# A hybrid HGRN2, Hyena and ConvFFN step: the value projection split around the first head's tiles, the recurrence's steps four half products earlier

## The chip, the core and the metric

The kernel runs on one core of a Trainium2 chip. Its metric is the device time of one execution in microseconds (us). The engines of the core work side by side and wait for each other on semaphores: TensorE (PE, whose weight loads the profile counts as PEld), VectorE (DVE), ScalarE (ACT), GpSimd (POOL) and SyncE (SP), which issues most of the transfers.

## What is computed

One layer of a diffusion backbone over 640 tokens: 512 sample tokens (a grid of 8 rows of 64) and 128 prompt tokens, with width 1024, all in float32. Cut to what matters:

```python
mod = silu(cvec) @ ada_w + ada_b                    # sh1, sc1, g1, sh2, sc2, g2
h = rmsnorm(x, norm1_w) * (1 + sc1) + sh1
q, ff, fb, iv, g, hy = split(h @ w_in)              # 5 x 512 columns, then 3 x 512
# HGRN2, 4 heads of 128 x 128, forward and backward
S = diag(f) S + k v^T;  o = S^T q                   # f from ff or fb, v from iv
o_hg = rmsnorm_per_head(o_f + o_b) * hg_norm_w * silu(g)
# Hyena, 512 channels
v, x1, x2 = split(dwconv3(hy))
u = x1 * v;  z = long_conv(u, kern) + hy_d * u      # by a Fourier transform
y_hy = rmsnorm(x2 * z) * hy_norm_w
x = x + g1 * (concat(o_hg, y_hy) @ w_out)
h = rmsnorm(x, norm2_w) * (1 + sc2) + sh2
gate, val = split(dwconv3(h @ ffn_w_up))            # 2 x 2816 columns
x = x + g2 * ((silu(gate) * val) @ ffn_w_down)
y = rmsnorm(x, final_norm_w)
```

The outputs are `y` for both groups of tokens and the final states of the prompt's scans.

## The kernel before

**Products.** A float32 product is made of three passes with split operands: each operand is a high part (`_hi`) and the rest (`_lo`), and `split_product` (L1314 to L1316) multiplies high by high, low by high and high by low. A weight unit of 128 x 1024 comes into a ring of buffers `raw` by a transfer that SyncE issues (`fetch`, L487). ScalarE makes `w_hi` of it (`split_hi`, L577, the row L584) and VectorE `w_lo` (`split_lo`, L876, the row L884). There are four places for split units, so the split of unit n + 4 waits until TensorE is done with unit n. Each of the three engines runs a list of operations in an order written out by hand, and the calls of `split_hi` and `split_lo` are placed in it.

**Up to the second norm.** In the order of TensorE's list:
- The value projection (`token_major` at IV, L1437): token-major, four units with two products each for five tiles of 128 tokens, so 120 matmuls of 128 x 512 into the five banks of `V_BANKS`. ScalarE copies the banks to `vtok` (L683) when the last unit is done.
- The 28 input tiles of 128 columns, each in two half products of 320 tokens: half product n uses bank n % 3 and has 24 matmuls. For each of four heads a `q`, `ff`, `fb`, two `hy` and a `g` tile, and four `hy` tiles at the end. The recurrence of a head has 12 steps on TensorE (`step`, L1474), ScalarE (L685) and VectorE (`pass_k` L1039 and others); step j of head h stands behind half product 7 + 12h + j (`FIRST_STEP`, `step_at`, L438). Steps 0 to 6 are the levels of the scores, with keys `kc` copied by ScalarE (L690) and `QQ` and `KK` moved on by VectorE (L1063, L1048). The remaining adaLN products are also placed behind fixed half products (`ADA_QUAD`).
- The transposes of `u` (`turn_u`, L1533), its forward transform, the HGRN2 part of the output product, the inverse transform (four channels: eight products of a sample part, two of a prompt part that reads `Up`, L1627), with `sum_channels` (L1609) for the sums of squares, and the Hyena part of the output product (`mix`, L1639), a tile of tokens at a time.

**The second norm.** For each of five tiles of 128 tokens: VectorE adds the residual (`mix_tile`, L1214, three operations on 128 x 1024), ScalarE squares and roots (`norm_tile`, L788), VectorE takes the reciprocal (`norm_row`, L1227 on), ScalarE scales to `xn` (`scale_tile`, L795), TensorE transposes in eight pieces (`turn_tile`, L1658), ScalarE modulates the eight pieces to `hf` (`modulate_tile`, L803), and VectorE splits them (`split_tile`, L894).

**The FFN.** Three rounds of 8, 8 and 6 tiles of 128 columns for gate and value. A round has for each unit two half products (`ffn_halves`, L123, which gives the order; in the first round the first halves of the first three units come ahead of their second halves), on banks 5 to 7; ScalarE takes each out to `padf` (`spread`, L589 to L594), VectorE convolves (L903 on), multiplies and splits. Behind them are two down projections, token-major, of five banks each, which VectorE adds to `x` (`add`, L1255: the rows L1257 and L1258). `before_half` (L1679) says what TensorE waits for, or does, ahead of one of the first half products. Between down projections TensorE's first product into bank i waits for the add of bank i:

```python
for k in range(nf // 2):
    split_lo(unit + LEAD_FFN)
    unit += 1
for i in range(NT):
    eng.wait_ge(sem("down_made"), (2 * r + n) * NT + i + 1)
    add(i, n, "down_taken", "x1_ready")
```

## Time and profile before

| | |
|---|---|
| median of three runs | 989.09 us (986.1 to 990.16) |
| the profiled execution | 991.46 us |
| its span, first to last instruction | 989.7 us |
| mean granted TensorE clock | 0.983 |
| PE busy | 941.6 us (95%), 5588 matmuls |
| PEld busy | 828.3 us (84%) |
| DVE busy | 629.1 us (64%) |
| ACT busy | 347.4 us (35%) |
| POOL busy | 14.1 us (1%) |
| DMA | 99.06 MB, mean 100 GB/s |

A share of busy time is an average over stages with different limits. TensorE is busy nearly throughout, so the time can change by what is left of its idle time, by the clock that it is granted (1.00 is 2.4 GHz, 0.50 is 1.2 GHz), and by the number of its instructions. The list of what it waited for tells which engine's order ended each wait.

The stages in the trace, in us from the span's start: the value projection 78.9 to 106.9, the 56 half products with the recurrence from 106.9, the HGRN2 part of the output product 414.3 to 442.0, the inverse transform from 445.0, the Hyena part of the output product to 488.6, the first FFN half product at 502.8, and the last adds, the final norm and the stores to 989.7.

### The profile page before, as it was taken

How to read it: one execution, taken by the hardware profiler on the slowest of the kernel's cores; microseconds unless marked ns; L12 is line 12 of the kernel's file. 1: busy time of each engine (PE TensorE's matmuls, PEld its weight loads, DVE VectorE, ACT ScalarE, POOL GpSimd, SP SyncE). 2: the span in 40 equal slices, each digit the busy share in tenths (PEclk: the TensorE clock that was granted, in tenths of full speed). 3: DMA queues.
4: the chain of work that ended last, by engine and by line, in shares of the span. 5: the costliest groups of instructions: out<-in, count | busy, mean ns of one | idle time of the engine just before them, and what ended most of it. 6: DMA issues, size and time to landing. Idle time of an engine off the chain costs nothing.

```text
span 989.7 us, 13758 instructions
## 1 busy us (share of the span) xinstructions
PE 941.6 (95%) x5588; PEld 828.3 (84%) x5588; DVE 629.1 (64%) x811; ACT 347.4 (35%) x614; POOL 14.1 (1%) x25
## 2 busy tenths in 40 slices
PE   6789999999999999989879999989999998999996
PEld 1247999899889899578769999878999986899985
DVE  4875258596695786896665766443756644466655
ACT  2362434333433333232473333211343321133332
POOL 0000000000000000001000000000000000000000
PEclk9899999999999999999989999999999999999998
DMA  8545144324422443115031221212122132112102
GB/s 284 217 175 167 65 150 128 101 77 149 134 97 100 129 128 123 64 43 192 1 126 66 86 86 65 91 58 85 65 72 78 64 106 65 64 64 86 43 1 106
DMA packets 27366, 99.06 MB, mean 100 GB/s; under 512 B 3271, under 2 KB 3655, under 8 KB 26536
## 3 DMA queue, kind: packets, MB, share of 16 engines
q1 hardware_dynamic: 25240, 89.06, 26.6%
q0 software_dynamic: 2064, 9.13, 2.7%
q8 instruction: 44, 0.72, 0.3%
q14 instruction: 18, 0.15, 0.1%
HBM read 95.01 MB, written 3.16 MB: 99 GB/s over the span
## 4 chain that ended last, share of the span: by engine, by line
PE 83%; DVE 10%; ACT 4%; issue 2%; DMA 1%; SPq 0%; DVEq 0%; ACTq 0%
PE ps L1314 23%; PE ps L1316 23%; PE ps L1315 23%; PE ps L1491 4%; PE ps L1332 2%; PE ps L1351 1%; PE ps L1627 1%; ACT hf L809 1%; DMA raw<-in_slots 1%; PE ps L1503 1%; PE ps L1586 1%; DVE h_lo L892 1%; DVE w_lo L884 1%; PE ps L1342 1%; PE ps L1511 1%
## 5 line engine op out<-in xcount | busy, mean ns | idle before, releaser
L1314 PE MATMUL ps<-h_hi,w_hi 128*128 128x320 f32 x1152 | 362.5, 315 | 3.7 <-DVE w_lo L884 3.7
L1315 PE MATMUL ps<-h_lo,w_hi 128*128 128x320 f32 x1152 | 357.6, 310 | 0.0
L1316 PE MATMUL ps<-h_hi,w_lo 128*128 128x320 f32 x1152 | 357.6, 310 | 0.0
L884 DVE TENSOR_TENSOR w_lo<-raw,w_hi 128x1024 fp32r<-128x1024 f32 x106 | 129.7, 1225 | 151.3 <-ACT w_hi L584 147.1
L1314 PEld LDWEIGHTS ps<-h_hi,w_hi 128*128 128x128 f32 x1152 | 218.2, 189 | 6.1 <-issue 4.3
L1315 PEld LDWEIGHTS ps<-h_lo,w_hi 128*128 128x128 f32 x1152 | 218.1, 189 | 0.1
L1316 PEld LDWEIGHTS ps<-h_hi,w_lo 128*128 128x128 f32 x1152 | 217.8, 189 | 0.0
L584 ACT ACTIVATE w_hi<-raw 128x1024 fp32r<-128x1024 f32 x106 | 111.2, 1052 | 119.6 <-PE ps L1316 114.5
L1314 PE MATMUL ps<-w_hi,a_hi 128*128 128x512 f32 x220 | 86.7, 394 | 6.3 <-DVE tmpd L1257 6.3
L1315 PE MATMUL ps<-w_lo,a_hi 128*128 128x512 f32 x220 | 86.4, 393 | 0.0
L1316 PE MATMUL ps<-w_hi,a_lo 128*128 128x512 f32 x220 | 86.2, 392 | 0.0
L1314 PEld LDWEIGHTS ps<-w_hi,a_hi 128*128 128x128 f32 x220 | 41.7, 189 | 16.4 <-issue 7.1
L903 DVE TENSOR_SCALAR cf<-padf,vec 128x648 f32<-128x648 f32 x44 | 24.5, 556 | 40.7 <-ACT padf L594 40.6
L1316 PEld LDWEIGHTS ps<-w_hi,a_lo 128*128 128x128 f32 x220 | 41.7, 190 | 8.8
L1315 PEld LDWEIGHTS ps<-w_lo,a_hi 128*128 128x128 f32 x220 | 41.7, 189 | 8.4
L1314 PE MATMUL ps<-w_hi,h_hi 128*128 128x512 f32 x120 | 48.1, 401 | 0.0
L1316 PE MATMUL ps<-w_hi,h_lo 128*128 128x512 f32 x120 | 46.8, 390 | 0.0
L1315 PE MATMUL ps<-w_lo,h_hi 128*128 128x512 f32 x120 | 46.7, 389 | 0.0
L851 ACT ACTIVATE a_hi<-actf 128x640 fp32r<-128x640 f32 x22 | 16.3, 741 | 80.1 <-DVE actf L1285 80.1
L1491 PEld LDWEIGHTS ps<-QQ,kc 128*128 128x128 f32 x280 | 35.9, 191 | 10.1 <-issue 10.1
L1491 PE MATMUL ps<-QQ,kc 128*128 128x128 f32 x280 | 39.3, 288 | 2.7 <-issue 2.7
L904 DVE SCALAR_TENSOR_TENSOR cf<-padf,vec,cf 128x648 f32<-128x648 f32 x44 | 39.3, 894 | 1.6
(254 smaller groups left out, 1047.8 us busy)
## 6 DMA issues: line engine op xcount, KB each, us to landing
raw<-in_slots SPq DMA_DIRECT2D x154, 512.0 KB, 3.7
xin<-in_x_sample SPq DMA_DIRECT2D x4, 512.0 KB, 5.8
xres<-in_x_sample POOLq DMA_DIRECT2D x4, 512.0 KB, 5.1
grow<-gates POOLq DMA_DIRECT2D x2, 1024.0 KB, 6.9
out_y_sample<-x SPq DMA_DIRECT2D x4, 512.0 KB, 3.1
decay<-in_decay SPq DMA_DIRECT2D x1, 1280.0 KB, 12.0
ktab<-in_ktab SPq DMA_DIRECT2D x1, 1024.0 KB, 5.7
tab<-in_utab POOLq DMA_DIRECT2D x1, 1024.0 KB, 7.5
```

Source lines behind the costliest of these rows:

```text
L584: A(w_hi[:, n % SPLITS, :], src, ACT.Copy).then_inc(sem("hi_ready"), 1)
L809: last = A(hf2[:, i % 2, k * P:(k + 1) * P], ps[:, TURN_BANKS[i] + k // 4, k % 4 * P:(k % 4 + 1) * P], ACT.Identity, scale=gain[:, 1, k, s ...
L851: A(a_hi[:, f, :], actf[:, :], ACT.Copy).then_inc(sem("ahi_ready"), 1)
L884: V.tensor_tensor(w_lo[:, n % SPLITS, :], raw[:, r % RING, :], w_hi[:, n % SPLITS, :].bitcast(F32), ALU.subtract).then_inc(sem("lo_ready"), 1)
L892: link(V.tensor_tensor(h_lo[:, k, :], buf, h_hi[:, k, :].bitcast(F32), ALU.subtract), "h_split")
L903: link(V.tensor_scalar(out, pad[:, 1:1 + CONV], taps[1], None, ALU.mult))
L904: link(V.scalar_tensor_tensor(out=out, in0=pad[:, 0:CONV], scalar=taps[0], in1=out, op0=ALU.mult, op1=ALU.add))
L1314: mm(out, lhs[0], rhs[0], start=first, stop=False)
L1315: mm(out, lhs[0], rhs[1], start=False, stop=False)
L1316: return mm(out, lhs[1], rhs[0], start=False, stop=last)
L1332: last = mm(ps[g * GROUP:(g + 1) * GROUP, bank, :], silu_c[:, GROUPS * j + g, :], piece[:, g % 2 * HW:(g % 2 + 1) * HW], start=(j == 0), s ...
L1491: last = mm(chunk(j, c), kc[:, l % 2, c * P:(c + 1) * P], ap(QQ, c * P, [(2 * s, P // (2 * s)), (T + s, 2), (1, s)]), start=True, stop=True)
```

## The change

Everything is done by the same arithmetic in the same numbers; what moves is the order on the engines, with the banks and semaphores that this needs.

- The value projection is made in two parts (`value_units`): units 0 and 1, then the six half products of head 0's `q`, `ff` and `fb`, then units 2 and 3, in which steps 0 to 2 of head 0 stand (`FIRST_AT`). The steps of all heads move up by four half products (`FIRST_STEP` 7 to 3). Head 0 has no `hy` tiles; six of them stand at the end, and the transposes of `u` stand between these.
- The adaLN products behind half products move along (`ada_half`).
- The inverse transform has its sample and prompt parts apart (`z_sample`, `z_prompt`); the sample parts of the first channels stand ahead of what reads `Up`, and the sums of squares stand later. VectorE makes the last two splits of the output weights behind the chain of `Up`.
- The second norm has another order on all three engines. For tiles 1, 2 and 4 VectorE takes four of the eight modulated pieces (`modulate_rest`). `mix` of tiles 3 and 4 is done in two halves of the columns. ScalarE squares into a buffer of its own (`junk2`).
- The first FFN round begins with the first halves of four units instead of three.
- In each down projection VectorE's last split of a weight unit stands behind the five adds.

The core of the diff:

```diff
 HY_TILES = [3 * _c + _what for _c in range(NC) for _what in (0, 1)] + [3 * _c + 2 for _c in range(NC)]
+_at_hy = iter(HY_TILES)
...
-    TILES += [("q", _g), ("ff", _g), ("fb", _g), ("hy", HY_TILES[2 * _g]), ("hy", HY_TILES[2 * _g + 1]), ("g", _g)]
-TILES += [("hy", _i) for _i in HY_TILES[2 * HEADS:]]
+    TILES += [("q", _g), ("ff", _g), ("fb", _g)] + [("hy", next(_at_hy)) for _ in range(2 if _g else 0)] + [("g", _g)]
+TILES += [("hy", _i) for _i in _at_hy]
...
-FIRST_STEP = 7
+FIRST_STEP = 3
+HEAD_TILES = 3
+HEAD_STEPS = 2 * HEAD_TILES - FIRST_STEP
...
-    first = 3 if r == 0 else 0
+    first = 4 if r == 0 else 0
     return [(u, half) for half in range(2) for u in units[:first]] + [(u, half) for u in units[first:] for half in range(2)]
...
+def tile_unit(t):
+    return IV // 2 + t if t < HEAD_TILES else IV + t
+IV_UNITS = (0, 1, HEAD_TILES + 2, HEAD_TILES + 3)
...
-    i = e - ADA_EARLY
-    return 5 + 12 * (i // 2) + 5 * (i % 2)
+    i = e - ADA_EARLY + 1
+    return 1 + 12 * (i // 2) + 5 * (i % 2)
...
+            def first_steps():
+                split_hi(8)
+                for j in range(HEAD_STEPS):
+                    step(0, j)
+                    if j == 1:
+                        split_hi(9)
+                for i in range(NT):
+                    eng.wait_ge(sem("v_bank"), i + 1)
+                    A(vtok[:, i, :], ps[:, V_BANKS[i], :], ACT.Copy).then_inc(sem("v_ready"), 1)
...
             for n in range(NH):
+                if n == 2 * HEAD_TILES:
+                    first_steps()
+                if n > FIRST_TURN:
+                    take_u(n - FIRST_TURN - 1)
                 kind, i = TILES[n // 2]
                 half = n % 2
                 c0 = half * HT
...
+                  scale=knorm[:, 1, c:c + 1]).then_inc(sem("z_taken"), 1)
+                eng.wait_ge(sem("zp_made"), c + 1)
...
+        junk2 = sb(norm2, "junk2", [D])
...
-                for k in range(KD):
+                if i >= 2:
+                    eng.wait_ge(sem("h_split"), KD + i - 1)
+                for k in range(KD // 2 if i in SHARED else KD):
...
             norm_tile(0)
             scale_tile(0)
             norm_tile(1)
-            scale_tile(1)
             modulate_tile(0)
             norm_tile(2)
+            scale_tile(1)
             scale_tile(2)
             modulate_tile(1)
+            split_hi(UNIT_FFN)
             modulate_tile(2)
-            split_hi(UNIT_FFN)
+            split_hi(UNIT_FFN + 1)
             norm_tile(3)
+            split_hi(UNIT_FFN + 2)
             scale_tile(3)
-            split_hi(UNIT_FFN + 1)
+            eng.wait_ge(sem("padf_zero"), 1)
+            take_half(NH, 0, 0, 0)
+            norm_tile(4)
+            split_hi(UNIT_FFN + 3)
             modulate_tile(3)
-            norm_tile(4)
             scale_tile(4)
-            split_hi(UNIT_FFN + 2)
+            take_half(NH + 1, 0, 1, 0)
             modulate_tile(4)
-            split_hi(UNIT_FFN + 3)
-            eng.wait_ge(sem("padf_zero"), 1)
...
+                if n == 2 * HEAD_TILES - 1:
+                    split_lo(8)
+                    for j in range(HEAD_STEPS):
+                        pass_k(0, j)
+                        step(0, j)
+                        if j == 1:
+                            split_lo(9)
...
-            for k in range(2):
-                split_lo(UNIT_WOUT + 4 + k)
...
+            for k in range(2):
+                split_lo(UNIT_WOUT + 4 + k)
...
+            def modulate_rest(i):
+                s = int(i == NT - 1)
+                eng.wait_ge(sem("x_turned"), 2 * i + 2)
+                for k in range(KD // 2, KD):
+                    link(V.tensor_scalar(hf2[:, i % 2, k * P:(k + 1) * P], ps[:, TURN_BANKS[i] + 1, k % 4 * P:(k % 4 + 1) * P],
+                                         gain[:, 1, k, s:s + 1], mod[:, 3 * KD + k, s:s + 1], ALU.mult, ALU.add),
+                         "h_rest" if k == KD - 1 else None)
...
             mix_tile(0)
+            mix_tile(1)
             norm_row(0)
-            mix_tile(1)
+            mix_tile(2)
             norm_row(1)
-            mix_tile(2)
             split_tile(0)
             norm_row(2)
+            modulate_rest(1)
+            modulate_rest(2)
+            split_tile(1)
+            split_lo(UNIT_FFN)
+            split_tile(2)
+            split_lo(UNIT_FFN + 1)
             mix_tile(3)
-            split_tile(1)
-            split_tile(2)
-            split_lo(UNIT_FFN)
+            split_lo(UNIT_FFN + 2)
             norm_row(3)
             mix_tile(4)
-            split_lo(UNIT_FFN + 1)
+            split_lo(UNIT_FFN + 3)
+            norm_row(4)
             split_tile(3)
-            norm_row(4)
-            split_lo(UNIT_FFN + 2)
+            modulate_rest(4)
             split_tile(4)
-            split_lo(UNIT_FFN + 3)
...
-                    for k in range(nf // 2):
+                    for k in range(nf // 2 - 1):
                         split_lo(unit + LEAD_FFN)
                         unit += 1
...
                         if last_half and 0 < i < NT - 1:
                             final_norm(i - 1)
+                    split_lo(unit + LEAD_FFN)
+                    unit += 1
...
+        FIRST_AT = ((2, 3), (3, 1), (3, 4))
...
+            def first_steps(p, i):
+                if (p, i) in FIRST_AT:
+                    step(0, FIRST_AT.index((p, i)))
...
+            def value_units(ps0, after):
+                for p in ps0:
+                    hi, lo = unit_ready(IV_UNITS[p])
+                    for i in range(NT):
+                        for kk in range(2):
+                            k = 2 * p + kk
+                            before_v(p, i, k)
+                            last = split_product(ps[:, V_BANKS[i], :], [x[:, k, i * P:(i + 1) * P] for x in (h_hi, h_lo)],
+                                                 [x[:, kk * HW:(kk + 1) * HW] for x in (hi, lo)], k == 0, k == KD - 1)
+                        if p == IV - 1:
+                            last.then_inc(sem("v_bank"), 1)
+                        elif i == NT - 1:
+                            last.then_inc(sem("unit_done"), 1)
+                        after(p, i)
...
+            value_units((0, 1), lambda p, i: None)
             for n in range(NH):
-                if n < 3:
-                    eng.wait_ge(sem("v_ready"), V_BANKS.index(n) + 1)
-                else:
+                if n == 2 * HEAD_TILES:
+                    value_units((2, 3), first_steps)
+                if 2 * HEAD_TILES <= n < 2 * HEAD_TILES + 3:
+                    eng.wait_ge(sem("v_ready"), V_BANKS.index(half_bank(n)) + 1)
+                elif n >= 3:
                     eng.wait_ge(sem("half_free"), n - 2)
-                if n == 3:
+                half_product(n, tile_unit(n // 2), n % 2)
...
+                if n == FIRST_TURN:
                     eng.wait_ge(sem("u_ready"), NC)
+                    eng.wait_ge(sem("rms_ready"), HEADS)
...
+            eng.wait_ge(sem("up_ready"), 1)
+            z_sample(0)
+            z_sample(1)
+            z_prompt(0)
+            z_sample(2)
+            z_prompt(1)
+            z_sample(3)
+            eng.wait_ge(sem("raw_taken"), 2 * NT)
+            sum_channels(0)
+            z_prompt(2)
+            sum_channels(1)
+            z_prompt(3)
...
             mix(2)
             turn_tile(0)
-            eng.wait_ge(sem("ysum_ready"), 1)
-            mix(3)
+            mix(3, (0,))
+            eng.wait_ge(sem("h_full"), KD + 1)
+            mix(4, (0,))
             turn_tile(1)
             turn_tile(2)
-            eng.wait_ge(sem("h_full"), KD + 1)
-            mix(4)
+            mix(3, (1,))
+            mix(4, (1,))
 
...
-                if at in (0, 3):
-                    eng.wait_ge(sem("h_split"), KD + (3, 5)[at // 3])
+                if at == 0:
+                    eng.wait_ge(sem("h_split"), KD + 3)
                 if at == 1:
-                    turn_tile(3)
                     eng.wait_ge(sem("mixed_taken"), 4)
                 if at == 2:
+                    turn_tile(3)
+                if at == 3:
                     turn_tile(4)
+                if at == 4:
+                    eng.wait_ge(sem("h_split"), KD + NT)
```

**VectorE at the first down projection's boundary** (`w_lo` is a weight split, `tmpd` and `x` are the two operations of an add). Before:

```order
L1284 TENSOR_TENSOR actf<-cf 128x512
L1285 TENSOR_TENSOR actf<-cf 128x128
L1287 TENSOR_TENSOR a_lo<-actf,a_hi 128x640
L884 TENSOR_TENSOR w_lo<-raw,w_hi 128x1024 x5
L1257 TENSOR_TENSOR tmpd<-ps,grow 128x512
L1258 TENSOR_TENSOR x<-x,tmpd 128x512
```

Now:

```order
L1341 TENSOR_TENSOR actf<-cf 128x512
L1342 TENSOR_TENSOR actf<-cf 128x128
L1344 TENSOR_TENSOR a_lo<-actf,a_hi 128x640
L922 TENSOR_TENSOR w_lo<-raw,w_hi 128x1024 x4
L1314 TENSOR_TENSOR tmpd<-ps,grow 128x512
L1315 TENSOR_TENSOR x<-x,tmpd 128x512
```

Four more pairs of adds follow in both. The first of the splits in the row belongs to the last unit of the half products; one of the others has moved behind the adds.

**VectorE in the second norm** (L1222 or L1266 is the first operation of a mix tile, L898 or L936 of a split tile, the reciprocal that of a norm). From the third mix tile on, before:

```order
L1222 SCALAR_TENSOR_TENSOR x<-ps,rhy,x 128x2x512
L1224 TENSOR_TENSOR x<-x,grow 128x2x512
L1225 TENSOR_TENSOR x<-x,xres 128x2x512
L898 CAST h_hi<-hf 128x8x128
L899 TENSOR_TENSOR h_lo<-hf,h_hi 128x8x128
L1230 RECIPROCAL stat<-stat 128x1
L1222 SCALAR_TENSOR_TENSOR x<-ps,rhy,x 128x2x512
```

Now:

```order
L1266 SCALAR_TENSOR_TENSOR x<-ps,rhy,x 128x2x512
L1268 TENSOR_TENSOR x<-x,grow 128x2x512
L1269 TENSOR_TENSOR x<-x,xres 128x2x512
L1274 RECIPROCAL stat<-stat 128x1
L936 CAST h_hi<-hf 128x8x128
L937 TENSOR_TENSOR h_lo<-hf,h_hi 128x8x128
L1274 RECIPROCAL stat<-stat 128x1
L1285 TENSOR_SCALAR hf<-ps,gain,mod 128x128 x8
L936 CAST h_hi<-hf 128x8x128
L937 TENSOR_TENSOR h_lo<-hf,h_hi 128x8x128
L922 TENSOR_TENSOR w_lo<-raw,w_hi 128x1024
```

The fourth mix tile stood behind one split; it now stands behind three splits of tiles, eight modulated pieces and two weight splits (the rows go on with the third split, a `w_lo` and the mix tile), and a third `w_lo` stands between it and its reciprocal.

**ScalarE at the value projection** (`vtok` are the value banks' copies, `qs` the first of head 0's `q`, `TT` and `KK` its gates and keys, `kc` the keys of a level). Before:

```order
L584 ACTIVATE w_hi<-raw 128x1024 x5
L683 ACTIVATE vtok<-ps 128x512 x5
L584 ACTIVATE w_hi<-raw 128x1024
L721 ACT_TABLE_LOAD
L721 ACTIVATE qs<-ps 128x320 x2
L584 ACTIVATE w_hi<-raw 128x1024
```

Now, from the last gate of head 0 on:

```order
L764 ACTIVATE TT<-ps 128x320
L765 ACTIVATE KK<-ps 128x320
L604 ACTIVATE w_hi<-raw 128x1024
L707 ACTIVATE kc<-KK 128x640 x2
L604 ACTIVATE w_hi<-raw 128x1024
L707 ACTIVATE kc<-KK 128x640
L735 ACTIVATE vtok<-ps 128x512 x5
L604 ACTIVATE w_hi<-raw 128x1024
L758 ACT_TABLE_LOAD
L758 ACTIVATE gs<-ps 128x320
```

The copies of the value banks stood ahead of head 0's tiles; they now stand behind the keys of its first three levels.

## Rows read from the trace of the kernel before

**Rows 1.** What PE waited for: us in total, times, longest

```profile
PE ps L1314 <- DVE tmpd L1257: 6.3, 2, 3.2
PE ps L1662 <- ACT xn L800: 5.1, 2, 2.7
...
PE ps L1314 <- DVE w_lo L884: 3.7, 2, 2.4
...
PE ps L1627 <- DVE Up L1180: 2.9, 1, 2.9
```

**Rows 2.** Windows: us, busy PE, PEld, DVE, ACT, POOL, granted clock, DMA, GB/s

```profile
445.03:450.04 5.01, 5.01 (x16) 4.20 (x17) 0.00 (x0) 0.00 (x0) 3.13 (x6) 0.70 0.68 238
450.49:453.94 3.45, 3.45 (x18) 3.04 (x17) 2.08 (x4) 1.18 (x3) 0.00 (x0) 1.00 1.05 430
502.82:507.88 5.06, 5.06 (x24) 5.06 (x25) 4.92 (x4) 2.06 (x2) 1.00 (x2) 0.68 0.32 104
...
517.20:625.55 108.35, 108.35 (x721) 108.35 (x721) 68.82 (x84) 41.17 (x82) 0.00 (x0) 0.97 0.24 78
685.00:797.63 112.63, 112.63 (x769) 112.63 (x768) 74.18 (x92) 39.24 (x77) 0.00 (x0) 1.00 0.22 71
625.55:652.94 27.39, 27.39 (x122) 22.34 (x120) 9.05 (x10) 5.37 (x7) 0.00 (x0) 1.00 0.29 96
656.10:685.00 28.90, 28.90 (x121) 23.77 (x121) 9.79 (x12) 3.18 (x3) 0.00 (x0) 0.94 0.22 73
828.18:855.78 27.60, 27.60 (x121) 22.29 (x121) 9.78 (x12) 3.18 (x3) 0.00 (x0) 1.00 0.24 77
```

**Rows 3.** Timeline at a down boundary: start, length, engine, [idle before, releaser]

```profile
654.12 1.23 DVE L884 TENSOR_TENSOR w_lo<-raw,w_hi 128x1024 fp32r<-128x1024 f32 x1 [5.57 <-ACT w_hi L584]
655.27 0.68 DVE L1257 TENSOR_TENSOR tmpd<-ps,grow 128x512 f32<-128x512 f32 x1
...
656.10 0.63 PE L1314 MATMUL ps<-w_hi,a_hi 128*128 128x512 f32 x1 [3.16 <-DVE tmpd L1257]
```

**Rows 4.** Timeline of DVE ahead of the inverse transform

```profile
437.83 2.36 DVE L884 TENSOR_TENSOR w_lo<-raw,w_hi 128x1024 fp32r<-128x1024 f32 x2
```

**Rows 5.** Timeline of DVE, the first channel of the inverse transform

```profile
451.75 0.89 DVE L1199 SCALAR_TENSOR_TENSOR zc<-u_hy,vec,zc 128x640 f32<-128x640 f32 x1 [6.87 <-ACT zc L777]
...
455.82 1.23 DVE L884 TENSOR_TENSOR w_lo<-raw,w_hi 128x1024 fp32r<-128x1024 f32 x1
```

**Rows 6.** Timeline of DVE, last mix tile to last split tile

```profile
502.78 1.28 DVE L1222 SCALAR_TENSOR_TENSOR x<-ps,rhy,x 128x1024 f32<-128x1024 f32 x1
...
506.62 1.22 DVE L884 TENSOR_TENSOR w_lo<-raw,w_hi 128x1024 fp32r<-128x1024 f32 x1
...
512.19 1.23 DVE L899 TENSOR_TENSOR h_lo<-hf,h_hi 128x1024 fp32r<-128x1024 f32 x1
```

**Rows 7.** Timeline of ACT, last tile of the second norm

```profile
513.64 1.15 ACT L800 ACTIVATE xn<-x,stat 128x1024 f32<-128x1024 f32 x1 [0.86 <-DVE stat L1230]
...
515.65 2.88 ACT L809 ACTIVATE hf<-ps,mod,gain 128x128 f32<-128x128 f32 x8
```

**Rows 8.** Groups of DVE: busy us, mean ns of one | idle before

```profile
L1079 DVE SCALAR_TENSOR_TENSOR states<-states,TU,ps 128x128 f32<-128x128 f32 x16 | 5.6, 348 | 0.6
```

**Rows 9.** Timeline, first convolution of the FFN and fifth unit's first half

```profile
527.72 0.56 DVE L903 TENSOR_SCALAR cf<-padf,vec 128x648 f32<-128x648 f32 x1 [5.95 <-ACT padf L594]
...
549.97 0.42 ACT L589 ACTIVATE padf<-ps 128x320 f32<-128x320 f32 x1
```

**Rows 10.** Timeline of DVE, head 0's first levels

```profile
145.51 1.42 DVE L1063 TENSOR_TENSOR QQ<-QQ,TT 128x640 f32<-128x640 f32 x1
...
148.73 0.83 DVE L1048 TENSOR_TENSOR KK<-KK,TU 128x640 f32<-128x640 f32 x1
```

**Rows 11.** Timeline of ACT: a value bank's copy, a level's keys

```profile
101.74 0.60 ACT L683 ACTIVATE vtok<-ps 128x512 f32<-128x512 f32 x1 [0.30 <-PE ps L1316]
...
149.59 0.74 ACT L690 ACTIVATE kc<-KK 128x640 f32<-128x640 f32 x1 [1.19 <-DVE KK L1048]
```

More of the change, by code:

```diff
@@ L111 @@
 NSLOT = _s
-UNIT_TILE = IV
 UNIT_WOUT = IV + len(TILES)
@@ L200, in token_major @@
         out.append((name, value))
-    token_major(IV, "v_bank", NT)
-    out.extend(("half_made", 2 * t + 2) for t in range(len(TILES)))
+    halves = [("half_made", 2 * t + 2) for t in range(len(TILES))]
+    out += [("unit_done", 1), ("unit_done", 2), *halves[:HEAD_TILES], ("unit_done", 3), ("v_bank", NT), *halves[HEAD_TILES:]]
+    plain = IV - 1
     out.extend(("hg_mixed", NT * (n + 1)) for _, n, _ in WOUT_UNITS[:4])
@@ L811, in modulate_tile, with take_half @@
                 last.then_inc(sem("h_full"), 1)
+            def take_half(n, t, gv, half):
+                eng.wait_ge(sem("half_made"), n + 1)
+                if t >= 2 and half == 0:
+                    eng.wait_ge(sem("fconv"), 2 * (t - 2) + gv + 1)
+                spread(ps[:, half_bank(n), 0:HT], padf[:, t % 2, gv, :], half, "half_free")
             norm_tile(0)
@@ L838, in _ @@
                     t = t0 + f
[L839 to L842 removed]
+                    if n >= NH + 2:
+                        take_half(n, t, gv, half)
                     n += 1
```

154 lines of the change are left out of this document (73 added, 81 removed).

## The prediction

> **What bounds the kernel now.** I read the list of what TensorE waited for first: nearly all of its idle time behind the first 60 us stands in four lines [rows 1]. Two waits of 3.2 us are for the first add of a down projection; the transposes of the second norm wait 2 x 2.7 us at most for `xn`; the first FFN products wait for `w_lo`; the inverse transform waits 2.9 us for `Up`. Elsewhere TensorE is fed, so nothing that only moves work there can gain. The windows [rows 2] add what a wait costs afterwards: sixteen inverse-transform products take 5.01 us at a granted clock of 0.70 behind their wait, where the next sixteen and their neighbours take 3.45 at 1.00. Behind the two down waits the same 120 products take 28.90 (0.94) and 27.60 (1.00) against 27.39 for the half before. So a wait may or may not bring the lower of the clock's two levels (1.2 GHz), and costs 0.2 to 1.7 us more. The rest is read where the waits are: VectorE's own order of work.
>
> I sum against the profiled execution, 991.46 us with a span of 989.7; it lies 2.4 above the median of 989.09, so the difference is taken over to the median. About 0.5% (5 us) can be told from no change.
>
> **1. The two down boundaries.** VectorE makes the `w_lo` of four units and then does the adds. The last unit's slot is free only when TensorE has finished the half, so `w_lo` starts at 654.12, the first add at 655.27 and TensorE at 656.10 [rows 3]. With the last `w_lo` behind the adds, the adds start while the last unit is still being multiplied: a product is 27.39/120 = 0.228 us, a tile of the last unit six, 1.37; a pair of adds is 1.44 (twice 0.69 and two gaps), so the adds keep up to within 1 us and never hold the next half, which takes its banks 1.37 apart. The moved `w_lo` is wanted four units (27 us) later: nothing. Saved: twice 3.16 plus 0.17 of overlap with the product before, and 1.5 and 0.2 of slow clock (28.90 and 27.60 less 27.39, and 0.17 each since the first half's end laps over): 5.0 + 3.7 = **8.7**. The third round's second half has no such wait, and saves nothing. Bounds: 6.7 (the waits alone) and 10.0 (both followed by the slow level).
>
> **2. The inverse transform.** The channels' first product no longer waits for `Up`. VectorE has its last input at 437.8 [rows 4], TensorE is in the output product until 441.97 (the start at 445.03 less the 2.9 wait and the overlap), so the products start 3.1 earlier and at full clock. That is not what comes out: the prompt part of channel 0 now stands behind two channels of products, 441.97 + 2 x 3.45 + 0.5 = 449.3, and ScalarE's copy 0.6 later. VectorE's channel then runs from 449.95, where it ran from 451.75 [rows 5]: 1.8 earlier. A channel is 4.0 of VectorE, and the first two carry a `w_lo` of 1.2 (451.75 to 455.82 and 1.23): 18.3 in all, so the fourth `y_split` comes at 468.2. TensorE waits for the third and fourth (1.2 and 1.4), and the sums of squares end at 470.75; VectorE's first mix tile starts at 472.1, which was 473.5: **1.4** net, of 3.1 in sight.
>
> **3. The second norm, up to the FFN.** A mix tile is 3.84 of VectorE (502.78 to 506.62), a split tile 1.96 (0.69 and the 1.23 of the row) [rows 6]; on ScalarE `xn` takes 1.15, eight modulate pieces 2.88 [rows 7], square and root 1.5 (from the tile's end to `xn` less the waits). Mix tiles 0 and 1 now run back to back, tile 2 ends at 485.6, and its norm no longer waits for a split. `modulate_rest` puts four pieces per shared tile on VectorE at 0.36 (0.35 and a gap, the nearest VectorE operation on a 128 x 128 piece of PSUM [rows 8]). The split of tile 2 ends at 497.8, and the first half product starts at 497.9, where it started at 502.82 [rows 2]. Then it turns: mix tile 3 ends at 502.85, but VectorE's next `w_lo` (third FFN unit) waits until ScalarE has done norm 3 and then this unit's `w_hi` (505.3), and the norm's reciprocal stands behind it, at 506.75. `xn` 3 is there at 508.0: TensorE, with two half products done at 504.9, waits 3.1. The same again: mix tile 4 to 510.6, norm 4, `w_hi`, eight pieces, `xn` 4 at 517.05: TensorE waits 4.7 more, the fourth half product starts at 517.9 (the third started at 517.20), the last split ends at 521.5 and the fifth half starts between 521.5 and 523 by the clock; I take 522.4.
>
> What the Trainium skill says against this part: "Advanced Engine Details and Errata", TRN2 Errata, has VectorE and ScalarE pay their memory latency as a bubble between instructions, advises large tiles, and puts ScalarE closer to PSUM; by it, four small pieces from PSUM are dearer on VectorE than on ScalarE, and at twice the price three shared tiles would add 4.3 us to VectorE's chain. The trace does not bear this out: 0.348 a piece on VectorE [rows 8] against 2.88/8 = 0.36 on ScalarE [rows 7].
>
> **4. The FFN's lead-in.** With four first halves instead of three, four units come to their convolutions 3.5 us apart. From the first convolution to the taking of the first half of the fifth unit VectorE and ScalarE need 549.97 - 527.72 = 22.25 us [rows 9]. From the fifth half's start at X the convolution starts at X + 4.2 and that half is taken by X + 26.9; TensorE wants its bank at X + 24.6 (seven times 3.52, which is 112.63/32 [rows 2]): a new wait of **2.3**. Twenty-one halves follow: the round's halves end at 522.4 + 26.9 + 73.9 = 623.2. Before: 625.55. Parts 2 to 4 together: **-2.35**. Bounds: -5.5 (no slow clock, X = 521.5, and no lead-in wait) and +1.5 (two spells of slow clock inside the waits' tails).
>
> **5. The value projection and head 0.** TensorE's instructions are the same, in another order; the split weights of both parts are made while three tiles run. Steps 0 to 2 of head 0 fit their slots: `qk_next` comes 4.5 after the last half product, the slot at 5.4. But ScalarE now copies level 2's `kc` before the five value banks, and that waits for VectorE: level 0 (148.73 - 145.51 = 3.2 [rows 10]), a `w_lo` of 1.2, then `pass_k` 0.83 [rows 10], from the end of step 1. That is 5.3, plus `kc` 0.74 and the first copy 0.60 [rows 11]: 6.7. TensorE has three value tiles (4.1) and step 2 (1.2) in that time, and half product 6 needs that copy: **+1.7**, a wait that was not there before. Bounds: 0, and 3.4 with a slow spell of 1.7.
>
> **6. The rest of the shift.** Head 0 has two tiles fewer and the steps start four halves sooner, so for each later head the steps meet the same tiles as before; the ada products keep their places beside the steps. The six last hyena tiles bring VectorE some 41 us of work in twelve slots of four: covered. The transposes of `u` now stand between half products; before they stood partly behind the last one, but TensorE was fed there too. The joins still wait for the last half product. 0, and if that cover were gone, up to 1 us per head.
>
> Sum: -8.7 - 2.35 + 1.7 = -9.35, so 989.09 - 9.35 = **979.7**.
>
> **The rivals.**
> A, the forecast: 979.7. Chance 0.5.
> B, the second norm's stage gains more: VectorE's chain is as I have it, but no slow clock follows the longer waits and the lead-in wait is hidden. For it: 27.60 at full clock behind a wait of 3.2 us [rows 2]. Against: two of three such waits were followed by the slow level. -8.7 - 5.5 + 1.7: 976.6. Chance 0.2.
> C, only the down boundaries gain, and the new waits of parts 3 to 5 (1.7, 3.1, 4.7, 2.3) cost what parts 2 and 3 give and a slow spell more: -8.7 + 1.5 + 1.7 = -5.5: 983.6. Chance 0.2.
> D, the shift does more than it says: ending the recurrence four halves early takes VectorE's last head off the way to the joins, where it stood at the end (a reciprocal of the whole head). Against: the joins wait for TensorE's tables product. At most 4 us more, the length of that reciprocal: 975.7. Chance 0.05.
> E, slower than before: the clock. The change makes many short waits of few long ones; I count eight (0.8, 1.2, 1.4, 1.7, 1.9, 2.3, 3.1, 4.7). The round-0 stretch in which two stood ran its 30 halves in 108.35 at 0.97 where 105.6 would be full speed: 2.8 lost behind one spot. If six of the eight cost that much and none is hidden by the chain it waits for, +16.8 - 9.35: 996.5; it decides from four on (11.2 against 9.35), slower by over 0.5% from six. Against: the longest two are tails of VectorE's chain, which a slow product only fills. Chance 0.05.
>
> **How the numbers follow.** Faster by over 0.5% (below 984.1): A, B, D and most of C: 0.88. Within 0.5%: the rest of C and the mild end of E: 0.08. Slower: 0.04. Range: A's terms move by 1.3 at the boundaries, by 3 in the norm, by 1.7 at the values, and B and C lie within: 975.5 to 984.5. Outside are E and the ends of C and D.
>
> **What would show it.** Right: no wait for the add of the down projection in TensorE's list; no wait for `Up`; a wait of some 1.7 us of TensorE for `vtok` before half product 6; two waits for `xn` of about 3 and 4.7 us with the fourth half product at its old place; one wait of 2 us for `padf` in the FFN's first ten halves. Wrong: waits per step of the recurrence, a down boundary that still waits, or a granted clock well under 0.98 over the run.

## The result, and the profile after

| | before | changed |
|---|---|---|
| median | 988.91 us (4 runs, 986.1 to 990.16) | 1000.58 us (4 runs, 996.47 to 1002.27) |
| the profiled execution | 991.46 us, span 989.7 | 999.02 us, span 997.2 |
| mean granted clock in it | 0.983 | 0.984 |
| PE busy | 941.6 us | 947.5 us |

The ratio is 1.0112, 95% interval 1.0069 to 1.0156: **slower by 1.1%**, where 979.7 was forecast and nothing above 984.5 was in the range. Below, what TensorE waited for in the changed kernel (the list of waits; us in total, times, longest), the answer to [rows 1]:

```profile
PE ps L1664 <- DMA tab<-in_utab: 7.7, 1, 7.7
PE ps L1761 <- ACT xn L829: 5.6, 2, 4.4
...
PE ps L1373 <- DVE h_lo L937: 2.5, 1, 2.5
PE ps L1373 <- ACT padf L609: 2.2, 1, 2.2
...
PE ps L1373 <- ACT vtok L735: 1.3, 1, 1.3
```

The waits for the adds and for `Up` are gone. At the top stands a wait that the kernel before did not have: the first product of the forward Fourier transform of `u` waits 7.7 us for its table, a transfer that GpSimd issues. The stages as windows of the changed kernel (columns as in [rows 2]): up to the HGRN2 part of the output product, that product, on to the first FFN product, the first round's half products, its two down projections, the second round, its down projections, the rest; then the transform and the fourth FFN half product.

```profile
81.70:429.36 347.66, 334.64 (x2219) 298.47 (x2217) 227.75 (x289) 121.84 (x194) 9.67 (x13) 0.99 0.33 109
429.36:457.01 27.65, 27.65 (x123) 22.69 (x121) 26.72 (x29) 8.31 (x12) 0.00 (x0) 1.00 0.16 57
457.01:514.62 57.61, 54.37 (x266) 45.88 (x264) 42.64 (x66) 24.91 (x50) 3.15 (x6) 0.94 0.28 105
514.62:641.85 127.23, 119.40 (x784) 118.64 (x785) 82.33 (x100) 50.06 (x99) 1.05 (x2) 0.96 0.23 86
641.85:696.28 54.43, 54.43 (x242) 45.07 (x241) 24.83 (x30) 9.61 (x11) 0.00 (x0) 1.00 0.25 87
696.28:808.92 112.64, 112.64 (x770) 112.64 (x768) 70.24 (x87) 39.23 (x77) 0.00 (x0) 1.00 0.20 71
808.92:863.34 54.42, 54.42 (x242) 45.05 (x241) 24.84 (x30) 9.62 (x11) 0.00 (x0) 1.00 0.25 87
863.34:997.20 133.86, 125.46 (x757) 118.08 (x755) 81.36 (x105) 44.85 (x94) 0.00 (x0) 0.99 0.16 59
411.82:428.21 16.39, 16.39 (x33) 7.29 (x34) 7.38 (x7) 2.74 (x4) 0.00 (x0) 0.85 0.06 23
535.20:541.00 5.80, 5.80 (x28) 5.80 (x27) 3.56 (x6) 1.49 (x6) 0.00 (x0) 0.63 0.00 0
```

The same stages of both kernels, each from TensorE's first instruction to the next stage's, give where the 7.5 us between the two spans come from:

| stage | before | changed | difference |
|---|---|---|---|
| up to the value projection | 79.02 | 81.70 | +2.68 |
| value projection to the HGRN2 output product | 335.31 | 347.66 | **+12.35** |
| that product to the first down projection | 211.22 | 212.49 | +1.27 |
| down projections, first round | 59.45 | 54.43 | -5.02 |
| half products, second round | 112.63 | 112.64 | 0.0 |
| down projections, second round | 58.15 | 54.42 | -3.73 |
| the rest | 133.92 | 133.86 | -0.06 |

The first row isn't the change's: two early groups of four products each took 3.8 us where they took 2.0, and so they did in one profiled execution of an unchanged start (the eleventh run below begins its value projection at 82.08, the third, the same kernel, at 79.06). The second row is the loss. GpSimd's list there (its timeline) is, in the kernel before:

```profile
366.83 1.79 POOL L540 DMA_DIRECT2D gates<-mod  x2 [46.06 <-DVE mod L947]
377.18 0.56 POOL L529 DMA_DIRECT2D tab<-in_utab  x1 [8.55 <-PE ps L1498]
385.24 0.71 POOL L529 DMA_DIRECT2D out_new_state<-newst  x1 [7.50 <-DVE newst L1083]
393.50 0.58 POOL L529 DMA_DIRECT2D ptab<-in_ptab  x1 [7.55 <-PE ps L1520]
```

and in the changed kernel:

```profile
394.86 1.80 POOL L560 DMA_DIRECT2D gates<-mod  x2 [86.12 <-DVE mod L985]
396.64 0.56 POOL L549 DMA_DIRECT2D tab<-in_utab  x1
397.20 0.71 POOL L549 DMA_DIRECT2D out_new_state<-newst  x1
397.90 0.58 POOL L549 DMA_DIRECT2D ptab<-in_ptab  x1
```

Ahead of the table's load stands the store of the second residual gate, two transfers of 1024 elements of 4 bytes (the expectation of run 1 says 512), which waits for the last adaLN block (`mod`). Before, the gate was out 10 us ahead of what the table itself waits for, the last head's step 8. Now that step is done early, but the last adaLN block comes 28 us later. The load is issued at 396.64 and lands 15.1 later, where TensorE had been ready at 404.1. The transform that follows ran at a granted clock of 0.85: 16.39 us.

### The profile page after: what moved, and what is told of

Its sections match the earlier page's. It is cut to its first block, busy times and chain, and to the rows that moved or that the text cites. A ratio compares the mean times of both kernels' runs of the same rounds, so it can differ in the third digit from the quotient of the medians.

```text
span 997.2 us, 13758 instructions
## 1 busy us (share of the span) xinstructions
PE 947.5 (95%) x5588; PEld 831.0 (83%) x5588; DVE 634.2 (64%) x823; ACT 342.1 (34%) x602; POOL 14.1 (1%) x25
## 4 chain that ended last, share of the span: by engine, by line
PE 80%; DVE 11%; ACT 3%; DMA 3%; issue 2%; POOL 0%; SPq 0%; ACTq 0%; DVEq 0%
PE ps L1373 22%; PE ps L1375 22%; PE ps L1374 21%; PE ps L1566 3%; PE ps L1391 2%; PE ps L1410 2%; PE ps L1664 2%; DMA tab<-in_utab 2%; PE ps L1705 1%; DMA raw<-in_slots 1%; DVE w_lo L922 1%; DVE o_hg L1126 1%; PE ps L1578 1%; DVE h_lo L930 1%; ACT hf L840 1%
## 5 line engine op out<-in xcount | busy, mean ns | idle before, releaser
L1566 PEld LDWEIGHTS ps<-QQ,kc 128*128 128x128 f32 x280 | 35.9, 191 | 10.5 <-issue 10.3
## 6 DMA issues: line engine op xcount, KB each, us to landing
decay<-in_decay SPq DMA_DIRECT2D x1, 1280.0 KB, 10.4
tab<-in_utab POOLq DMA_DIRECT2D x1, 1024.0 KB, 15.1
```

The costliest lines, as they stand in the source:

```text
L1566: last = mm(chunk(h, j, c), kc[:, l % 2, c * P:(c + 1) * P], ap(QQ, c * P, [(2 * s, P // (2 * s)), (T + s, 2), (1, s)]), start=True, stop= ...
```

## The experiments

Each ratio is to runs of the kernel before on the same chip. Three theories at first: **Q**, the loss is GpSimd's queue, in which the table's load stands behind the store; **S**, the shift itself would put another wait at the same place; **C**, the loss is many short waits and the clock behind them. The runs stand here by what they test, numbered as they were made.

**1. The gate's store behind the tables.**

```diff
-            gate_out(1)
             eng.wait_ge(sem("head_steps"), (HEADS - 1) * STEPS + KTURN + 1)
...
             load(ptab[:, :, :, :], io["ptab"][:, 1:3], "ld_ptab")
+            gate_out(1)
```

> The changed kernel with one move on GpSimd's list: the store of the second gate (two transfers of 512 elements each, wait for the last adaLN block) stands behind the loads of the Fourier table and of the prompt's table, not ahead of them. Theory Q (the queue): the changed kernel loses its time because the table's load stands behind that store in GpSimd's list; it was issued at 396.6 and landed at 411.8, TensorE had been ready at 404.1, waited 7.7 us and made the transform at a granted clock of 0.85 (16.4 us where 13.8 would do). By Q the wait for the table is gone and the run is 10.3 shorter than the changed kernel: 990 by its median of 1000.6, 987 by its profiled run. Theory S (the shift itself: the last head's end or the splits take over as the next wait at the same place): a new wait of 5 us or more ahead of the second part of the transform, 996 to 998. Theory C (many short waits and the clock, no single place): within 2 us of the changed kernel, 999 to 1001.

Measured: 988.23, ratio 0.9962 (0.9937 to 0.9988), span 989.6. GpSimd's timeline, and the window from the transform to the output product:

```profile
365.41 0.59 POOL L549 DMA_DIRECT2D tab<-in_utab  x1 [56.63 <-PE ps L1572]
...
394.93 1.77 POOL L560 DMA_DIRECT2D gates<-mod  x2 [10.23 <-DVE mod L984]
```

```profile
403.99:419.04 15.05, 15.05 (x38) 6.68 (x37) 10.82 (x11) 4.13 (x8) 0.57 (x1) 1.00 0.15 30
```

The table is issued 31 us earlier and no wait takes its place. From the value projection to the output product: 337.08 against 347.66, 10.6 shorter, 7.7 of it the wait and 2.5 the clock (17.54 against 15.05 from the transform's start). Q holds for this stage (it had 10.3), S and C fall. The whole profiled execution is 7.6 shorter, not 10.6: between the output product and the first FFN half product it took 59.90, where the changed kernel's took 57.61 in the same order.

**2. The wait kept, the gate's packets behind the table's load.**

```diff
-            gate_out(1)
-
+            eng.wait_ge(sem("mod_ready"), ADA_ORDER.index(11) + 1)
             eng.wait_ge(sem("head_steps"), (HEADS - 1) * STEPS + KTURN + 1)
             eng.wait_ge(sem("scores_taken"), HEADS * 8)
             load(tab[:, :].rearrange("p (a b c d) -> p a b c d", a=2, b=2, c=2), io["utab"], "ld_tab")
+            gate_out(1)
```

> The changed kernel, with GpSimd still waiting for the last adaLN block ahead of the table's load, but with the store of the gate (1024 elements of 4 bytes) issued behind that load. It splits theory Q in two. If the gate's small packets ahead in the same queue made the table's landing take 15.1 us where it took 7.5 in the kernel before: the table is issued at about 395 and lands at 402.5, just ahead of TensorE's 404.1, so the time is that of the first run of this job (990 or 987). If the landing was slow for another reason (other traffic): it lands at 410, TensorE waits 6 us, and the time is within 2 us of the changed kernel's.

Measured: 994.89, ratio 1.0037 (1.0016 to 1.0058), between the two times that were expected. The load was issued at 392.15 and landed at 407.1; TensorE waited 5.7. So that the packets stand ahead in the queue is not what makes the landing slow.

**5. The wait kept, the store far away** (behind the inverse table's load).

```diff
-            gate_out(1)
-
+            eng.wait_ge(sem("mod_ready"), ADA_ORDER.index(11) + 1)
             eng.wait_ge(sem("head_steps"), (HEADS - 1) * STEPS + KTURN + 1)
...
             load(tab[:, :].rearrange("p (a b c d) -> p a b c d", a=2, b=2, c=2), io["itab"], "ld_tab")
+            gate_out(1)
```

> The changed kernel, with GpSimd waiting for the last adaLN block ahead of the Fourier table's load as in the changed kernel, but with the gate's store (1024 elements of 4 bytes) far away, behind the load of the inverse table. In the run with the store right behind the table's load the load still took 15.0 us, so its order in the queue was not what made it slow. Theory N (the small packets near it, before or behind, take the engines' time): the table, issued at 392 to 395, lands in 5 to 7.5 us, by 402, TensorE (ready at 401.5 to 404) waits under 1 us, and the ratio to the kernel before is that of the run with the store behind the tables, 0.996. Theory W (the wait alone, with whatever else moves at that time): it lands after 15 us, TensorE waits 5 to 6, ratio 1.003.

Measured: 985.81, ratio 0.9972 (0.994 to 1.0004); the load, issued at 394.66, landed in 8.0, and TensorE didn't wait. The view of the transfers in the 7.4 us behind the load's issue in the changed kernel, and in the 8 us behind it here:

```profile
DMA packets 134, 0.31 MB, mean 42 GB/s; under 512 B 80, under 2 KB 80, under 8 KB 115
...
tab<-in_utab POOLq DMA_DIRECT2D x1, 1024.0 KB, 15.1
raw<-in_slots SPq DMA_DIRECT2D x1, 512.0 KB, 13.8
```

```profile
DMA packets 466, 2.20 MB, mean 275 GB/s; under 512 B 60, under 2 KB 60, under 8 KB 337
...
tab<-in_utab POOLq DMA_DIRECT2D x1, 1024.0 KB, 8.0
raw<-in_slots SPq DMA_DIRECT2D x1, 512.0 KB, 5.0
```

Runs 2 and 5 differ in the place of the store alone, and the landing is 14.9 in one and 8.0 in the other. The slow spell comes a few us behind the store and takes SyncE's load of a weight in another queue too (13.8 against 5.0). In run 2 the 8 us behind the load's issue still carried 217 GB/s, and the 7 us after them (400 to 407) 48:

```profile
DMA packets 390, 1.73 MB, mean 217 GB/s; under 512 B 100, under 2 KB 100, under 8 KB 261
```

```profile
DMA packets 103, 0.33 MB, mean 48 GB/s; under 512 B 22, under 2 KB 22, under 8 KB 103
```

A load that has moved by then is spared: in run 5 the inverse table's load, 1 MB too, was issued 0.55 us ahead of the store and landed in 5.4. A load of SyncE's that came 3.1 us behind the store took 9.8. That the elements of 4 bytes are the cause is argued and not shown, since no run stores the gate in another form; a store as such isn't enough, for that of the last state, 128 KB, was issued 0.6 us behind the table's load in run 5 too.

The two halves of the fault are needed together: the wait put the load late by 29 us, for which there was just room, and the gate's packets beside it took 7 us more. The store beside an early load was not run; the table of run 1 landed over 33 us ahead of its use, which would hide it. The Trainium skill says on its page "DMA: Bandwidth & Descriptors", section "Queues, rings and completion order", that each DMA engine takes turns between queues packet by packet. That a load in another queue is slowed as well is in keeping with it.

**4. The fault alone, in the kernel before.**

```diff
+            eng.wait_ge(sem("head_steps"), HEADS * STEPS)
             gate_out(1)
-
-            eng.wait_ge(sem("head_steps"), (HEADS - 1) * STEPS + KTURN + 1)
```

> The kernel before with the fault alone: on GpSimd's list the wait for the last head's last step (393.0 in its trace) stands ahead of the gate's store and of the table's load. By theory Q the table is issued at 395, lands at 410 behind the gate's packets, TensorE waits 11 us from 398.8 on and loses some 2.6 to the clock: 1002.5. If the wait in the changed kernel was only a sign of something else that TensorE would have waited for anyway: 989 to 992.

Measured: 1003.28, ratio 1.0121 (1.0084 to 1.0158); a wait of 10.3 for the table, and 18.23 us from the transform to the output product where the kernel before has 15.49. Q again, with its price.

**3. The adds first, in the kernel before.**

```diff
-                    for k in range(nf // 2):
+                    for k in range(nf // 2 - 1):
...
+                    split_lo(unit + LEAD_FFN)
+                    unit += 1
```

> The kernel before with one part of the change: in each down projection VectorE's last split of a weight unit stands behind the five adds. By the forecast's own term: 8.7 less, 980.2 by the median of 988.9, with no wait for an add in TensorE's list. A rival: the boundary's time comes back later (the split that is made late, or a first half product that waits for it): 2 us or less gained, 987.

Measured: 983.04, ratio 0.9918 (0.9895 to 0.9941), 8.1 less. Its windows for the two pairs of down projections:

```profile
626.02:680.45 54.43, 54.43 (x243) 45.05 (x242) 24.84 (x30) 9.62 (x11) 0.00 (x0) 1.00 0.26 87
793.08:847.50 54.42, 54.42 (x242) 45.05 (x241) 24.83 (x30) 9.62 (x11) 0.00 (x0) 1.00 0.27 87
```

They are those of the changed kernel to 0.01 us, and nothing comes back later: the profiled span is 8.3 shorter.

The next five stand on run 1. One caution for all of them: the stretch from the inverse transform's start to the first FFN half product, in which they have one order, took 59.9 in runs 1, 2, 5, 6 and 12, but 58.24, 56.64, 56.72 and 56.66 in runs 7 to 10. Runs 9 and 12 are the same kernel, so up to 3 us there come from the execution and not from the edit.

**6. Value copies first.**

```diff
-                for j in range(HEAD_STEPS):
+                for j in range(HEAD_STEPS - 1):
                     step(0, j)
-                    if j == 1:
-                        split_hi(9)
+                split_hi(9)
                 for i in range(NT):
+                    if i == NT - 1:
+                        step(0, HEAD_STEPS - 1)
```

> The changed kernel with the gate's store behind the tables (the first run of the first job, 0.996 of the kernel before), and ScalarE's copies of the first four value banks ahead of the keys of head 0's level 2. By the forecast's part 5: TensorE's wait of 1.3 for a value bank ahead of the seventh half product is gone, 1.3 less, ratio 0.995, which is at the edge of what can be told, so the profile decides: value projection to the start of the HGRN2 output product 1.3 shorter. A rival: the keys come later and step 2 of head 0 waits in its place: same time.

Measured: 985.7, ratio 0.997 (0.9947 to 0.9994), not to be told from run 1 by time; the window from the value projection to the output product is 335.25 where run 1 has 337.08, and the wait for `vtok` is gone: 1.8.

**7. Another order in the second norm.**

```diff
             split_hi(UNIT_FFN + 1)
-            norm_tile(3)
             split_hi(UNIT_FFN + 2)
+            split_hi(UNIT_FFN + 3)
+            norm_tile(3)
             scale_tile(3)
...
-            norm_tile(4)
-            split_hi(UNIT_FFN + 3)
             modulate_tile(3)
+            norm_tile(4)
...
-            mix_tile(3)
             split_lo(UNIT_FFN + 2)
+            mix_tile(3)
+            split_lo(UNIT_FFN + 3)
             norm_row(3)
             mix_tile(4)
-            split_lo(UNIT_FFN + 3)
-            norm_row(4)
             split_tile(3)
+            norm_row(4)
```

> The changed kernel with the gate's store behind the tables (0.996 of the kernel before), and another order in the second norm: ScalarE splits the third and fourth FFN unit ahead of the norm of tile 3, VectorE the third ahead of mix tile 3 and the fourth ahead of its reciprocal, ScalarE modulates tile 3 ahead of the norm of tile 4. Theory O (the stage's lost gain is order on ScalarE and VectorE: two reciprocals stand behind a split that waits for a split on ScalarE): the waits of 1.2 and 4.4 for xn fall to 0.2 and 1.8, the fifth half product starts 5 earlier, ratio 0.991. A rival (the adds and splits of tiles on VectorE are the bound, whatever their order): 1 to 2 less, 0.9945.

Measured: 983.53, ratio 0.9931 (0.9901 to 0.996). From the inverse transform to the first down projection 183.07 (58.24 + 124.83) against 187.50 (59.90 + 127.60) in run 1: 4.4 less, of which 1.7 lie ahead of the first half product, where the order is the same, and 2.8 behind it. The waits for `xn` are 1.6 and 2.6, not 0.2 and 1.8: the two half products ahead of the first ran at full clock here (7.37 us, not 8.8), so TensorE was there sooner, and at the second VectorE's reciprocal stood behind the split of tile 3. So order gave some 2.8 us here, between the 5 and the 1 to 2 that were expected; by time the gain isn't clear, since the interval of run 6, on the same chip and without this order, overlaps (0.9947 to 0.9994).

**8. Runs 6 and 7 together.**

> The two before this together: gate's store behind the tables, value copies first, and the other order in the second norm. If their gains add: 1.3 + 5 less than the run with the store alone moved, ratio 0.990, which is below the kernel before with the adds first alone (0.992).

Measured: 983.05, ratio 0.9939 (0.9908 to 0.9971), short of the 0.990 expected and no better than run 7 by time. Its stages are 335.33, which is the gain of run 6, and 179.93, 3.1 below run 7 in the same order; half of that again lies ahead of the first half product.

**9. VectorE takes half of tile 3's pieces too** (on run 8).

```diff
-        SHARED = (1, 2, 4)
+        SHARED = (1, 2, 3, 4)
...
             mix_tile(4)
-            split_tile(3)
+            modulate_rest(3)
             norm_row(4)
+            split_tile(3)
```

> The run with the store behind the tables, value copies first and the other order in the second norm, and now VectorE also takes four of the eight modulated pieces of tile 3, right behind mix tile 4. In that run ScalarE was still at tile 3's pieces when mix tile 4 was ready, and TensorE waited 2.6 for xn of tile 4. If that ScalarE time is what it waited for: the wait falls to 1.1 and the fifth half product starts 1.5 earlier, ratio 0.001 to 0.002 below that run's 0.994. If VectorE's four pieces (0.44 each with the gap) hold the split of tile 3 and with it the fifth half product: no change in the end of the first round's half products.

Measured: 981.52, ratio 0.9887 (0.9854 to 0.9919). The longest wait for `xn` is 1.6, and that for tile 4 1.3; the wait that was to shrink did. The first half product to the first down projection took 122.62 against 123.29, but 121.09 in run 12, the same kernel, so those 0.7 can't be told from the spread.

**10. Three first halves** (on run 8).

```diff
-    first = 4 if r == 0 else 0
+    first = 3 if r == 0 else 0
...
                 if at == 3:
                     turn_tile(4)
-                if at == 4:
                     eng.wait_ge(sem("h_split"), KD + NT)
```

> The run with the store behind the tables, value copies first and the other order in the second norm, with three first halves instead of four in the first FFN round, as in the kernel before. By the forecast's part 4 the wait for padf of 2.2 ahead of the twelfth half product is the price of four first halves: it is gone here; in its place TensorE waits for the split of tile 4 ahead of the fourth half product, some 4 (split at 522.8 where it is at 518.9). Net 1.5 to 2 longer from the first half product to the first down projection. If the padf wait stays, part 4 read its cause wrongly.

Measured: 985.04, ratio 0.9916 (0.9884 to 0.9947), and 126.24 against 123.29 in that window, 2.95 longer. From its list of waits:

```profile
PE ps L1373 <- DVE h_lo L937: 6.4, 2, 3.9
```

No wait for `padf` is left in it, and one of 3.9 for the split of tile 4 has come: part 4 of the forecast read the cause rightly. By this window four first halves are worth their price; by time that isn't shown (run 8 has 0.9939).

**11 and 12. The adds alone beside the best version.** Run 11 is the kernel of run 3, run 12 that of run 9.

> The kernel before with the adds first, a second time, beside the best version of the changed kernel on the same chip. If the rest of the change is worth something once its faults are mended, this is the slower of the two by some 2 to 4 us; by the stages of their profiled runs, 4.4 shorter from the HGRN2 output product to the first down projection, against a start of the value projection that was 2.9 later. If it is worth nothing: both within 1 us.

> The changed kernel with the store behind the tables, value copies first, the other order in the second norm and tile 3 shared, a second time, beside the kernel before with the adds first on the same chip. See there: 2 to 4 us faster than it, or within 1.

Measured: 980.99, ratio 0.9896 (0.9858 to 0.9935), and 980.55, ratio 0.9905 (0.9878 to 0.9932). The same within 0.5 us: with its faults mended, all the rest of the change is worth nothing that can be told, though the intervals leave room for the 2 to 4 us that were expected. Their profiled executions took 335.47 and 335.28 from the value projection to the output product, and 209.72 and 208.61 from there to the first down projection. Both beat both kernels, and run 3's edit is one moved split.

## Why the prediction was wrong

The step that failed is in **part 6**: "the ada products keep their places beside the steps ... 0, and if that cover were gone, up to 1 us per head". The formula keeps them beside the steps, but the first block can no longer stand behind half product 1 (its bank, 3, still holds a value sum there), so every block takes the next place: the last one's products went from half products 46 and 47 to 49 and 50, while the last head's step 8 (its transposes of the keys, for which the table's load waits) went from 51 to 47. Who waits for that block is GpSimd, with the transform's table queued behind. I listed the engines that the steps feed and left out GpSimd's list and its transfers. The trace of the kernel before shows 10.4 us between the two and 14 between the table's landing (384.7) and its use (398.84); the price then came with the store. That too was to be seen before, at loads for which nothing waited: SyncE's were 3.7 us to landing as a median, but 9.3 for the one issued at 174.69, 5.3 us behind the first gate's store, and 7.4 for the one at 374.57, 7.7 us behind the second's. The step cost 10.6 in its stage (run 1). VectorE made it worse: `mod` stood behind the last head's division, a convolution and a weight split, 6.5 us after TensorE's last transpose for it (387.70):

```profile
384.61 4.15 DVE L1126 RECIPROCAL o_hg<-o_hg 128x640 f32<-128x640 f32 x1 [3.66 <-ACT o_hg L718]
...
392.11 0.89 DVE L944 SCALAR_TENSOR_TENSOR x<-padm,vec,x 128x648 f32<-128x648 f32 x1
393.04 1.23 DVE L922 TENSOR_TENSOR w_lo<-raw,w_hi 128x1024 fp32r<-128x1024 f32 x1
394.18 0.18 DVE L984 TENSOR_REDUCE mod<-ps 128x8 f32<-128x32 f32 x1
```

The other terms, by the profiled executions:

| part | forecast | measured |
|---|---|---|
| 1, down boundaries | -5.0 and -3.7 | -5.02 and -3.73 |
| 2 to 4, up to the first down projection | -2.35 | +1.27 |
| 5, value projection | +1.7 | +1.8 (run 6), of it a wait of 1.3 |
| 6, the rest of the shift | 0 | +10.6, and -0.1 without the queue |

The second row is that of one execution each. In runs 1, 2, 5 and 6, whose order there is the changed kernel's, the stretch took 215.1 to 215.2, which is +3.9; the kernel before's own took 207.3 in run 4 and 209.7 in run 11. Part 5's terms don't give its figure: 6.7 less 4.1 and 1.2 is 1.4, close to the wait of 1.3 that came.

**Part 1** was right in mechanism and size, and carried alone it gives 8.1 (run 3). VectorE's timeline in the changed kernel shows the order that did it: the last split of the half, the adds, the moved split.

```profile
690.83 1.23 DVE L922 TENSOR_TENSOR w_lo<-raw,w_hi 128x1024 fp32r<-128x1024 f32 x1 [5.57 <-ACT w_hi L604]
691.98 0.68 DVE L1314 TENSOR_TENSOR tmpd<-ps,grow 128x512 f32<-128x512 f32 x1
...
698.50 0.69 DVE L1315 TENSOR_TENSOR x<-x,tmpd 128x512 f32<-128x512 f32 x1
699.23 1.23 DVE L922 TENSOR_TENSOR w_lo<-raw,w_hi 128x1024 fp32r<-128x1024 f32 x1
```

**Parts 2 to 4** had the mechanism and missed sizes, as far as the profiled execution tells. Measured from the end of the HGRN2 output product, VectorE's first channel came where the sum put it (464.96 against 464.99) and so did the fourth `y_split` (483.2). Then three terms were too small. The sums of squares ended 1.0 late: TensorE's third sum stands behind 18 products, which took 6.61 us at a granted clock of 0.64, and ScalarE's last square waits for that sum:

```profile
476.70:483.31 6.61, 6.61 (x23) 5.26 (x22) 6.04 (x13) 1.71 (x4) 0.00 (x0) 0.64 0.19 69
```

VectorE's pieces were dearer than the row that I took for them:

```profile
505.40 1.51 ACT L840 ACTIVATE hf<-ps,mod,gain 128x128 f32<-128x128 f32 x4
505.91 3.54 DVE L1285 TENSOR_SCALAR hf<-ps,gain,mod 128x128 f32<-128x128 f32 x8 [1.80 <-PE ps L1761]
```

0.44 each against 0.36 forecast and 0.38 on ScalarE, 0.7 for the eight that stand ahead of the first half product. The page of the Trainium skill that the forecast sets against its row, "Advanced Engine Details and Errata", TRN2 Errata, which puts ScalarE closer to PSUM, has the right sign here, by a sixth and not by a factor of two. Together they make the first half product 57.6 behind the output product's end, where I had 55.9. And the clock: the fourth half product with its transposes took 5.80 at 0.63 behind the 4.4 wait, so the fifth started at 541.0 where the sum, moved to this execution, has 537.4. From there to the first down projection it took 100.85, where the sum has 100.8, so the 3.6 us between 537.4 and 541.0 are the whole miss of parts 2 to 4. The waits themselves were read well: 1.2 and 4.4 for `xn` (3.1 and 4.7 forecast; the first two half products took 8.83, not 7, and hid part of the first), 2.2 for `padf` (2.3), none for `Up`, none for an add. All of these were named as what would show the steps right, and came; only the fourth half product wasn't at its old place but 2.3 us behind it, counted from the output product's end; what would have shown the sum wrong, a wait for a transfer, was not on my list.

Rival E gave the right sign for the wrong reason: the mean clock is 0.984 against 0.983. The profiled executions give +7.5 for the change and the medians +11.7; between run 1 and the changed kernel they give 7.6, and the ratios 1.5% (some 15 us). So more is lost than the profiled stages show, and where the other executions lost it stays open.

## What to carry to other kernels

When steps are moved, list for every engine's queue, GpSimd's and SyncE's too, which waits stand ahead of which transfers, and compare for each wait how far its event moves with how far that of the thing behind it moves: here one went 4 places up and the other 3 down. A transfer that feeds the critical path should stand ahead of any store that waits for something else, and away from stores of single elements. And test the parts of a large reordering alone: one moved split gave all of the gain that could be told.

## What was not expected of the hardware

- A store of twice 1024 elements of 4 bytes, within about 2 us of a 1 MB load and on either side of it, about doubled the load's landing: 15.1 and 14.9 (changed kernel, run 2) and 14.0 (run 4) against 7.5 (before), 5.0 (run 1) and 8.0 (run 5). A 512 KB load in another queue, issued 5.3 us behind the store, took 13.8 against 5.0. One 1 MB load just ahead of the store was spared (5.4, run 5).
- Two operations of VectorE on the same 128 x 128 piece of PSUM cost differently: 0.345 to 0.348 for that which [rows 8] show, 0.410 for one with two operands per partition (changed kernel).
- Between executions of unchanged code the first 80 us differ by 3.0 (79.06 in run 3, 82.08 in run 11), with two groups of four products that took 3.8 or 2.0 each.
